# The third branch of a merge and the output projection by seven half products a pair, with the raw tokens turned inside a gate pair

## The reference, cut to what matters

```python
def merge(pr, o_a, o_b, o_c, w_proj_a, w_proj_b, w_proj_c, w_out):
    ga, gb, gc = (jax.nn.sigmoid(t) for t in pr[11:14])
    y = ga * (o_a @ w_proj_a) + gb * (o_b @ w_proj_b) + gc * (o_c @ w_proj_c)
    return y @ w_out
...
x = x + g_a * y_lat
x = x + g_f * expert_choice_ffn(modulate(x, norm2_g[l], sh_f, sc_f), ...)   # 16 experts, 1024 x 1024 matrices
```

## Time and profile before

| | us |
|---|---|
| median of 3 runs | 2857.53 (2853.68 to 2858.9) |
| the profiled execution | 2855.44 |
| its span in the trace | 2853.4 |
| PE busy | 2721.9 (95%) |
| DVE / ACT / POOL busy | 1197.8 / 524.6 / 116.8 |

### The profile page before, as it was taken

The page is one execution under the profiler, slowest core; times in us unless marked ns, Lnnn a source line. Parts: engine busy times, 40 slices in busy tenths (PEclk is TensorE's granted clock), DMA queues, the critical chain, the costliest instruction groups (busy, mean ns, idle before and its releaser), DMA issues.

```text
span 2853.4 us, 31371 instructions
## 1 busy us (share of the span) xinstructions
PE 2721.9 (95%) x12418; PEld 1750.1 (61%) x12418; DVE 1197.8 (42%) x2239; ACT 524.6 (18%) x876; POOL 116.8 (4%) x96
## 2 busy tenths in 40 slices
PE   7999999999899999999799999989989999999997
PEld 3688888887544444443344333334486787888886
DVE  4255565654444444212311111155273335754654
ACT  2122122122232332210100000031322103100001
POOL 1122221110000000000000000000000000000000
PEclk9999999999999999999899999989999999999998
DMA  9522121101111211323699999942102431333330
GB/s 354 197 59 59 51 59 52 47 26 37 52 45 45 59 45 45 95 82 111 268 409 409 409 409 409 409 118 67 36 1 74 118 90 30 89 89 89 89 89 30
DMA packets 327669, 374.53 MB, mean 131 GB/s; under 512 B 10033, under 2 KB 273030, under 8 KB 324230
## 3 DMA queue, kind: packets, MB, share of 16 engines
q1 hardware_dynamic: 327286, 371.93, 38.1%
q10 hardware_dynamic: 272, 1.05, 0.1%
HBM read 370.85 MB, written 2.10 MB: 131 GB/s over the span
## 4 chain that ended last, share of the span: by engine, by line
PE 91%; DVE 4%; DVEq 1%; DMA 1%; ACT 1%; SPq 1%; issue 1%; ACTq 0%
PE psum L1562 26%; PE psum L1877 12%; PE psum L1373 8%; PE psum L2033 6%; PE psum L1494 4%; PE psum L720 3%; PE psum L1113 2%; PE psum L1762 2%; PE psum L815 2%; PE psum L1532 2%; PE psum L728 2%; PE psum L2564 2%; PE psum L1803 2%; PE psum L705 2%; PE psum L1303 2%; PE psum L1352 1%
## 5 line engine op out<-in xcount | busy, mean ns | idle before, releaser
L1562 PE MATMUL psum<-arena 128*128 128x256 f32 x3528 | 773.3, 378 | 0.5 <-ACT arena L2662 0.5
L1562 PEld LDWEIGHTS psum<-arena 128*128 128x128 f32 x3528 | 662.8, 189 | 97.6 <-issue 3.9
L1877 PE MATMUL psum<-arena 128*64 128x512 f32 x1536 | 347.6, 597 | 3.0 <-issue 2.1
L1877 PEld LDWEIGHTS psum<-arena 128*64 128x64 f32 x1536 | 104.8, 136 | 217.6 <-issue 214.5
L1373 PE MATMUL psum<-arena 128*128 128x512 f32 x512 | 233.1, 597 | 0.0
L2033 PE MATMUL psum<-arena 128*128 128x512 f32 (+1 forms) x448 | 169.4, 536 | 0.0
L1373 PEld LDWEIGHTS psum<-arena 128*128 128x128 f32 x512 | 92.4, 189 | 104.1 <-issue 104.1
L1808 DVE SCALAR_TENSOR_TENSOR arena<-psum,arena 128x512 f32<-128x512 f32 x64 | 48.0, 750 | 246.4 <-PE psum L1803 245.8
L2033 PEld LDWEIGHTS psum<-arena 128*128 128x128 f32 x448 | 85.6, 191 | 83.3 <-issue 79.9
L1594 DVE TENSOR_TENSOR arena<-psum,arena 128x256 f32<-128x256 f32 x55 | 23.4, 425 | 250.0 <-ACT arena L1607 192.4
L1494 PE MATMUL psum<-arena 128*128 128x512 f32 x256 | 112.0, 592 | 1.7 <-DVEq L1397 1.7
(11 more groups left out here) (374 smaller groups left out, 3281.0 us busy)
## 6 DMA issues: line engine op xcount, KB each, us to landing
arena<-in_w_gate SPq DMA_DIRECT2D x64, 1024.0 KB, 18.2
arena<-in_w_up SPq DMA_DIRECT2D x64, 1024.0 KB, 16.1
arena<-in_w_down SPq DMA_DIRECT2D x64, 1024.0 KB, 17.8
arena<-in_w_in SPq DMA_DIRECT2D x120, 512.0 KB, 4.0
arena<-in_ada_w SPq DMA_DIRECT2D x24, 1024.0 KB, 7.4
arena<-in_w_up SPq DMA_DIRECT2D x32, 512.0 KB, 5.2
arena<-in_w_down SPq DMA_DIRECT2D x32, 512.0 KB, 5.0
arena<-in_w_out SPq DMA_DIRECT2D x16, 512.0 KB, 4.0
```

Of the source, the lines that this page charges most:

```text
L1562: mm = pe.matmul(psum[:, base + b, c * HALF:(c + 1) * HALF], w, v, start=(first and q == 0 and m in (0, 2, 3, 4)), stop=(last and q == KC ...
L1877: mm = pe.matmul(psum[64 * e:64 * e + 64, bank + n, :], tokens(e, 2 * q + k), w[:, k, 512 * n:512 * n + 512], start=(q == 0 and k == 0), s ...
```

## The change

The 16 units of the third branch and the first 6 of the output projection go in **eleven pairs** by `pe_seven`, in the order g0 g1 w0 g2 w1 g3 w2 w3 o0 o1 o2; the last two units of the output projection stay plain. Pairs use banks 0 to 3 and 4 to 7 in turns. POOL forms the weight sums of every pair (`pool_merge`), once both units have arrived. DVE forms token sums of cT before, and of each pair of y after its "w". The eight blocks of transposes of the raw tokens move into pair 1 (g1), half of them ahead of its third quarter and half ahead of its fourth; their load moves from before the first merge unit to after the fourth, and waits for the last `pe_values`. The raw tokens stay in a place of their own (`stream`) until the projection is added. The expert weights get another order of places.

```diff
+        MERGE = [("g", 0), ("g", 1), ("w", 0), ("g", 2), ("w", 1), ("g", 3), ("w", 2), ("w", 3), ("o", 0), ("o", 1), ("o", 2)]
...
+        for lo_, hi_, name, unit in ((16384, 20480, "merge", 15), (24576, 28672, "merge", 15), (20480, 24576, "w_out", 5),
+                                     (8192, 12288, "w_out", 5), (0, 8192, "w_out", 5)):
+            ws.last.append((lo_, hi_, ws.phases[name]["base"] + unit))
...
+        def pool_merge(pool):
+            for n in range(len(MERGE)):
+                name, u = merge_units(n)
+                for e in range(2):
+                    ws.arrived(pool, name, 0, u + e)
+                if n < 2:
+                    done(pool, "attn", 0, unit_of_fill(4 * KC - 3))
+                else:
+                    done(pool, merge_units(n - 2)[0], 0, merge_units(n - 2)[1] + 1)
+                weight_sums(pool, *merge_weights(n), merge_sums(n), "merge_sums")
...
         def pe_merge(pe):
-            for n, (kind, c) in enumerate(LAST_ORDER):
-                if n == 1:
-                    pe_values(pe, PAIRS_Q - 1)
...
+            pe.wait_ge(sem("gate_out"), FILLED)
+            pe_values(pe, PAIRS_Q - 1)
+            for n, (kind, c) in enumerate(MERGE):
...
+                pe.wait_ge(sem("merge_sums"), n + 1)
...
+                if n >= 2:
+                    pe.wait_ge(sem("merge_out"), n - 1)
...
+                if n == MERGE.index(("o", 0)):
+                    ready = lambda pe, q: pe.wait_ge(sem("yt_sums"), q + 1)
+                x, t = {"g": (HT[:, :, C:T], ht_t), "w": (cT, ct_t), "o": (yT, yt_t)}[kind]
+                pe_seven(pe, *merge_weights(n), merge_sums(n), x, t, 4 * (n % 2), True, True, ready)\
+                    .then_inc(sem("weights_used"), 2)
...
         def dve_merge(dve):
...
+                recombine(dve, 4 * (n % 2), mg_a[n % 2], mg_u, o)
+                dve.sem_inc(sem("merge_out"), 1)
+                if n == 0:
+                    for k in range(KC):
+                        dve_turn_stream(dve, k)
                 if kind == "w":
...
+                    dve.tensor_tensor(o, o, mg_gate[c % 2], ALU.mult)
+                    dve.drain()
+                    y = yT[:, pair, :]
+                    dve.tensor_tensor(y, y, o.rearrange("p (e n) -> p e n", e=2), ALU.add)
+                    dve.drain()
+                    token_sums(dve, y, yt_t[:, c])
+                    dve.sem_inc(sem("yt_sums"), 1)
...
-        SLOTS = [0, 1, 2, 3, 8, 9, 10, 11, 12, 13, 5, 6, 4, 7]
+        SLOTS = [4, 5, 8, 9, 12, 13, 10, 11, 6, 7, 0, 1, 2, 3]
...
+        BETWEEN = {"mod": {1: sp_setup_late}, "merge": {3: sp_x_again}, "experts": {SLOTS.index(0) - 1: sp_await_w_out}}
```

More of the change, by code:

```diff
@@ L157, in phase, with load @@
         self.total += n * iters
-    def load(self, eng, name, then=None, between=None):
+    def load(self, eng, name, then=None, between={}):
         ph = self.phases[name]
@@ L164, in load @@
             eng.dma_start(dst, src(0)).then_inc(self.full[ph["slots"][u]], 16)
-            if between and u == 1:
-                between(eng)
+            if u in between:
+                between[u](eng)
         if then:
@@ L1060, in mixed_block_kernel @@
                  [4 + n % 4 for n in range(len(sources))])
[L1061 to L1065, removed]
+        MERGE = [("g", 0), ("g", 1), ("w", 0), ("g", 2), ("w", 1), ("g", 3), ("w", 2), ("w", 3), ("o", 0), ("o", 1), ("o", 2)]
+        w_out1 = cut(A["w_out"][0], P)
+        units = [w_in_at("gc", 2 * c + e) if kind == "g" else (lambda i, c=2 * c + e: w_proj[2][c])
+                 for kind, c in MERGE if kind != "o" for e in range(2)]
+        ws.phase("merge", 1, [(w,) + unit_place(4 + n % 4) for n, w in enumerate(units)], [4 + n % 4 for n in range(2 * KC)])
+        ws.phase("w_out", 1, [((lambda i, n=n: w_out1[n]),) + unit_place(4 + n % 4) for n in range(KC)],
+                 [4 + n % 4 for n in range(KC)])
+        for lo_, hi_, name, unit in ((16384, 20480, "merge", 15), (24576, 28672, "merge", 15), (20480, 24576, "w_out", 5),
+                                     (8192, 12288, "w_out", 5), (0, 8192, "w_out", 5)):
+            ws.last.append((lo_, hi_, ws.phases[name]["base"] + unit))
         tail = Carve(arena, CT_LO, CT_LO + 4 * S)
@@ L1508, in dve_merge @@
+            act_square_chunk(act, n_ffn, KC - 2)
+            act_square_chunk(act, n_ffn, KC - 1)
+            act_root(act, n_ffn)
         def dve_merge(dve):
             dve_fill(dve, NSTEP - 1)
-            for n, (kind, c) in enumerate(LAST_ORDER):
-                if kind == "w":
[L1512 to L1516, removed]
@@ L1519, in residual @@
[L1519 to L1545, removed]
@@ new lines, in dve_merge, with dve_stream, sp_await_w_out @@
+            for e in range(2):
+                done(dve, "w_out", 0, KC - 2 + e)
+                dve_stream(dve, KC - 2 + e, psum[:, 4 + 2 * e, :])
+                for k in ((4, 5), (6,))[e]:
+                    dve_fold(dve, n_ffn, k)
+        def dve_stream(dve, k, branch):
+            dve.scalar_tensor_tensor(XT[:, k, :], branch, g_a[:, k:k + 1], stream[:, k, :], ALU.mult, ALU.add)\
+               .then_inc(sem("w_out_out"), 1)
+        def sp_await_w_out(sp):
+            sp.wait_ge(sem("w_out_out"), KC)
@@ L1613, in dve_quad @@
             dve.sem_inc(sem("quad_out"), 1)
[L1615 to L1623, removed]
         h2T = Carve(arena, HT_LO, HT_LO + 4096).take(KC, S)
         n_ffn = norm(XT, h2T, S, lambda k: scale2[:, k:k + 1], lambda k: mod[:, SH_F * KC + k, 0:1], 4,
-                     Carve(arena, EXTRA[0], EXTRA[1]).take(S), lambda k: ("w_out_out", 4 + k + 1), True)
+                     Carve(arena, EXTRA[0], EXTRA[1]).take(S), lambda k: ("w_out_out", k + 1), True)
         h2tok = yT.rearrange("p k n -> p (k n)").rearrange("p (t d) -> p t d", t=LT)
```

133 lines of the change are left out of this document (98 added, 35 removed).

## The result

| | before | changed |
|---|---|---|
| median of the runs taken together, us | 2857.99 | 2837.16 |
| ratio to before, 95% interval | | 0.9925 [0.991, 0.9941] |
| the profiled execution | 2855.44 | 2836.63 |
| its span | 2853.4 | 2834.8 |

In a second, later comparison the changed kernel's median was 2837.84 (five runs) against 2855.62, ratio 0.9934 [0.992, 0.9947]. The forecast was 2835.0. The two spans differ by 18.6 us.

The account below looks back on a forecast made before the run. PE was taken to bound the kernel, busy 2721.9 of 2853.4 us. Gross gain 22.5 - 0.4 - 0.4 = 21.7 gives 2833.7 from the profiled execution, 2835.8 from the median; forecast 2835.0, range 2832 to 2839.

Parts of the forecast that it names:

- Eleven pairs at 12.09: Merge's last third and output projection: 22 plain units, 152.0 us, become eleven pairs of 12.09, 133.0 us; gain 19.0.
- Two gaps closed, 3.56: At the merge's end, PE's two waits for DVE's gating, 1.64 and 1.92 us, go; gain 3.56.
- Stretch: Merge's last third and output projection, 178.20 us before: gain 21.7 us net, leaving about 156 to 158.
- Load and sums, 0.4: Pairs 2 to 10: PE waits for weight loads and POOL's sums, 0 to 4.5 us in all, taken as 0.4.
- the lower end: Pairs 2 to 10: load and sums take 10.9 us against a pair's 12.09, slack of 1.2, no wait.
- Pair 8's token sums, 0.4: Last quarter of pair 8: PE waits for DVE's token sums, 0 to 2.4 us, taken as 0.4.
- second rival: DVE and POOL block each other for whole instructions: waits of 2.1 in pair 8, 1.0 after four "w" pairs; 2841 us; chance 0.12.
- The first pairs, "Nothing": Start of the merge's last third: first pairs' loads, sums and raw tokens are ready in time, costing PE 0 us.
- Experts, nothing; cover 26: Start of the experts: their later first load costs nothing, since 26 us of cover remain.
- The slower case: Pairs 2 to 10: PE waits the chain's whole excess in all nine pairs; 10 us slower, 2868; chance 0.04.
- turning point, 2.5: Pairs 2 to 10: the gain is lost at 2.5 us of wait per pair, a load-and-sums chain of 14.6.

Follow-up runs that it names:

- e2_plain: Changed kernel's order, loads, places and banks, but every pair by plain matmuls, without weight or token sums; 2850.06 us, ratio 0.9978.
- e9_tokens_first: Changed kernel with POOL's pair 0 sums held until the last softmax is scaled, pair 9's until DVE has added into y; 2832.70 us, ratio 0.9919.
- e1_hold0: Changed kernel with POOL's weight sums of pair 0 held until attention's last softmax is scaled; 2833.81 us, ratio 0.9927.
- e6_both: Changed kernel with POOL's pair 0 sums held until the last softmax is scaled, pair 9's until the last token sums are done; 2835.25 us, ratio 0.9924.
- e11_hold0: Changed kernel with POOL's pair 0 sums held until the last softmax is scaled, run again in the later comparison; 2835.07 us, ratio 0.9928.
- e4_long: Changed kernel with POOL's first addition made three times for every pair from pair 2 on; 2844.14 us, ratio 0.9963.

## Why the prediction was right, step by step

- *Eleven pairs at 12.09.* Right: 238 records took 51.40 in the chain, 12.09 for 56. Plain units took 6.88 in e2_plain, not 6.91, so the seven products gave 11 x (13.75 - 12.09) = 18.3 for the 19.0 of the sum; the rest counts with the order.
- *Two gaps closed, 3.56.* Right. The order alone gave 4.2, these gaps and the 0.03 a unit above.
- *Stretch.* Forecast gain 21.7, measured 20.5 (and 157.8 us against 156 to 158).
- *Load and sums, 0.4.* Measured 0.2 in the changed kernel, in one pair of nine, and 0.3 to 0.6 in other profiles. In the other eight pairs the loads' landings and POOL's work stayed inside 12.09, as the lower end had it. The one is pair 6, in every profile of a kernel with weight sums of normal length: in the changed kernel its second load landed 6.1 us after its issue, where the sum had at most 5.9, and POOL began 6.8 us after the end of pair 4 (7.5 in e9_tokens_first) and took 5.3. Why this load is late is open.
- *Pair 8's token sums, 0.4.* Mis-sized: 1.21 in both profiles of the changed kernel. The step took 0.7 a token sum from a row in which DVE's operation was doubled. In truth DVE waits for the rest of POOL's operation, 1.07, 0.91 and 0.74 here. That is the second rival's mechanism, the rule of the Trainium skill (SBUF — State Buffer, "SBUF: two separate sides") read strictly, with 1.2 of the 2.1 us that it was priced at. Its second half, a wait of 1.0 behind each "w" pair, did not come at that size: behind pair 7 POOL's four operations took 5.4 us there (1283.70 to 1289.11) and still fitted.
- *The first pairs, "Nothing".* This step failed. It asked whether pair 0's sums are ready in time, and not whom they disturb: they are made while attention's last steps run, and cost 1.4 us there. The exclusion was looked for only between operations with two SBUF inputs; this one is a TENSOR_SCALAR with one. e1_hold0, e6_both, e9_tokens_first and e11_hold0 all take these 1.4 us away.
- *Experts, nothing; cover 26.* Nothing is right, 26 is not: it had all 14 loads landed before the first expert starts. PE needs them one by one, and the loads come at 409 GB/s.
- *The slower case.* Its price, the whole excess at each of nine pairs, was wrong by a factor of two, and it left out the clock. The two errors pull against each other. At an excess of 4.4 it said 40, and it was 26. At 1.9 (two waits of e4_long that follow each other add up to 1.5 to 2.1) it said 17, and it was 7.9. Its turning point, 2.5, is too low: the losses of the medians, 7 and 24, against the 18 that there were to lose put it near 3.5, an estimate on a straight line between the two kernels.

The whole is 18.6 against 21.7: 1.2 in the stretch (0.8 of it in pair 8), 1.4 in attention, the rest, 0.5, in what the change puts no work into. The mechanism of the gain is right, and 20.5 of its 21.7 us are measured where it was said to come. That the whole time, 2836.63 by the median of the three runs, came as near to 2835.0 as it did is in part luck: the 1.1 and 1.1 ahead of the step and in the router are all but offset by the 1.7 behind, and runs of this kernel lie 5 us apart.

## What to carry to other kernels

Before work is given to an idle engine, look at which instructions of its neighbour run at that moment, not only at whether the result comes in time: here 5.4 us of work on an idle POOL, done 18 us before it was needed, cost 1.4 us of PE time. Price a late helper that fills one of two buffers at half its excess for each round (so it was for 1.9 and 4.4 us here), and add the clock once the waits get long (here from 3.2 us). Let a semaphore decide the order of two engines that exclude each other, where one has slack and the other has none.

## What the runs showed of the hardware

- DVE and POOL, both on SBUF, took turns by whole instructions: TENSOR_SCALAR 128x768 took 1.62 and 1.40 for 0.62, TENSOR_TENSOR 128x512 took 1.76 for 0.69, and POOL's 128x512 took 1.77 for 1.27 when DVE had started 0.04 earlier. The first has only one SBUF input. The Trainium skill (SBUF — State Buffer, "SBUF: two separate sides") counts an operation of VectorE in a 2-port mode with those that exclude GpSimd; the trace doesn't say which mode ran.
- DVE's recombine, with an input in PSUM, ran beside POOL unhindered: 0.42, and 0.42 and 0.69 in e4_long (from 1217.50 and 1218.33, with a POOL addition from 1217.52 to 1218.61).
- Waits of 3.2 to 5.7 us in PE were followed by stretches with a granted clock of 0.89 to 0.93 (a mean over time at the 1.2 and the 2.4 GHz level), and e4_long's waits of up to 1.87 by 1.00. The lower clock made the same matmuls of the stretch some 8 us longer.
